# Weight halves kept in memory by block 0 and loaded by the seven later blocks

## The chip, the cores and the metric

One core of a Trainium2 chip runs the kernel. Its engines are TensorE (PE), VectorE (DVE), ScalarE (ACT), GpSimd (POOL) and SyncE (SP), which here only issues DMAs. The metric is device time in microseconds of one execution. Before the change it is 2832.45 us, the median of 3 runs (2832.03 to 2832.45).

## The reference

A layer of a streaming encoder over 4096 frames of 1024 features. All projections are in float32.

```python
mod = c_act @ ada_w[l] + ada_b[l]
shift, scale, gate = jnp.split(mod, 3, axis=-1)
h = rms_norm(x, norm_w[l]) * (1.0 + scale[:, None]) + shift[:, None]
p = h @ w_in[l]
gq, gk, gv, gz, glr, hq, hf, hi, hz, mg = jnp.split(p, IN_SPLITS, axis=-1)
# two chunked linear recurrences (64 frames a chunk) give o_g and o_h
g_a, g_b = jnp.split(jax.nn.sigmoid(mg + merge_b[l]), 2, axis=-1)
m = g_a * (o_g @ w_up_gla[l]) + g_b * (o_h @ w_up_hgrn[l])
x = x + gate[:, None] * (m @ w_out[l])
return rms_norm(x, final_norm_w)
```

`w_in` is 1024 by 5136, the two up projections are 512 by 1024 and `w_out` is 1024 by 1024. The weights are the same for every frame.

## The kernel before

The frames are cut into 8 blocks of 512. Each block walks through the same 66 slots. A slot is one piece of weights of 128 x 1024 (0.524 MB; slots 4 and 5 have 1088 columns) and the matmuls that use it: 24 of 512 columns in most slots, 48 of 272 columns in slots 4 and 5, and 12 in each of the 14 output slots 52 to 65 (`OUT0` is 52). Slots 0 to 27 are projections for the recurrences, 28 to 51 are merge gates (`MG_SLOT`) with the up projections among them (`UP_SLOT`). Smaller "hosted" matmuls for the recurrences stand between slots, mostly in slots 6 to 30.

For precision every weight w is split into two halves of the reduced type fp32r: `w_hi` is w rounded, and `w_lo` is w - `w_hi`. Activations are split in the same way, and each product is three matmuls, hi x hi, hi x lo and lo x hi (`PASSES`).

The weights pass through two sets of buffers. SyncE loads slot s into one of `RAW` = 4 buffers `w_raw` (`load_w`, L322 to L325). ScalarE copies it to `w_hi` (`split_hi`, L574), VectorE subtracts to `w_lo` (`split_lo`, L819), and TensorE reads both. The halves lie in a ring of `RING` = 3. ScalarE and VectorE therefore split slot s+3 at their own step s, just after TensorE has finished slot s (`slot_done`), and SyncE, which waits for `w_split` alone, runs some three slots ahead of TensorE and issues the raw load of slot s+4 once slot s is split. The other loads and stores of SyncE stand in the same program at fixed slots: x for the next block (`load_x`, `load_pair`), x for the residual (`xy`) and the stores of the result (`store_out`, L377).

The order of the work is written out by hand. Every engine has one in-order program, and they meet at semaphores. In ScalarE's step of a slot the copy of slot s+3 comes before most of the rest: activations, copies out of PSUM, and the small DMAs of `a_rows`, on which TensorE waits.

In block 0 GpSimd does one thing more (`out_pieces`, L473). It loads 8 pieces of `w_out`, multiplies them by the gate, forms their sums for a Strassen-like product, and stores 14 pieces to the scratch tensor `pieces` (L486). ScalarE waits for `pieces_out` in slot 21 of block 0 before it writes `o_tm`, which shares the memory of `w_b`; SyncE waits for it before the first load of a piece.

Of the kernel before, what the change touches and what calls it, by code (L numbers as in the profile page):

```python
# [14 lines left out]
P = 128  # L15
# [11 lines left out]
RAW, RING = 4, 3  # L27
SLOT_W = 4 * GW
# [13 lines left out]
OUT0 = _s  # L42
# [32 lines left out]
RAW_AT = [s % RAW if s < 20 else (s - 20) % 3 if s < 26 else (s - 26) % RAW for s in range(SLOTS)]  # L75
RAW_NTH = [RAW_AT[:s].count(RAW_AT[s]) for s in range(SLOTS)]
RAW_NEXT = [next(n for n in range(s + 1, 2 * SLOTS) if RAW_AT[n % SLOTS] == RAW_AT[s]) for s in range(SLOTS)]

# [4 lines left out]
def slot_width(s):  # L83
    return SLOT_W if GK0 <= s < I0 else 1024
# [13 lines left out]
def build(nc, x, xt, mod_in, cols, rows, w_stream, ada, out):  # L98
    fp32, f32r = mybir.dt.float32, mybir.dt.float32r
    ALU, ACT, AX = mybir.AluOpType, mybir.ActivationFunctionType, mybir.AxisListType  # L100
    NB = x.shape[0] // T

    ctx = ExitStack()
    with ctx:
# [126 lines left out]
        raw_in = [signal(f"raw_in{r}", RAW_AT.count(r) * 16) for r in range(RAW)]  # L231
        pieces = nc.dram_tensor("pieces", [PIECES, P, 1024], fp32, kind="Internal").ap()
        w_hi_done = signal("w_hi_done", SLOTS)
        w_split = signal("w_split", SLOTS)
# [86 lines left out]
        def _(sp):  # L321
            def load_w(s):  # L322
                r = RAW_AT[s]
                src = pieces[s - OUT0, :, :] if s >= OUT0 else w_stream[s, :, 0:slot_width(s)]
                sp.dma_start(w_raw[:, r, 0:slot_width(s)], src).then_inc(raw_in[r].sem, 16)  # L325
# [53 lines left out]
            def body(b, last, first=False):  # L379
                for s in range(SLOTS):  # L380
# [12 lines left out]
                    if s == 43 and not last:  # L393
# [3 lines left out]
                    if s in (50, 51) and not last:  # L397
                        sp.wait_ge(x_sq.sem, x_sq.at(b + 1, s - 47))
                        load_pair(b + 1, s - 50)
# [12 lines left out]
                    if s == 3 and not first:  # L412
                        store_out(b, -NT)
# [144 lines left out]
        def _(act):  # L558
# [10 lines left out]
            def split_hi(b, s):  # L569

                r = RAW_AT[s]
                act.wait_ge(raw_in[r].sem, raw_in[r].at(b, (RAW_NTH[s] + 1) * 16))
                n = slot_width(s)
                AF(w_hi[:, s % RING, 0:n], w_raw[:, r, 0:n], ACT.Copy).then_inc(w_hi_done.sem, 1)  # L574
# [70 lines left out]
            def body(b, last):  # L645
                link_at[0], link_at[1] = b, 0
                for s in range(SLOTS):
# [42 lines left out]
                    if not (last and s + RING >= SLOTS):  # L690
                        split_hi(b if s + RING < SLOTS else b + 1, (s + RING) % SLOTS)
# [113 lines left out]
        def _(dve):  # L805
# [10 lines left out]
            def split_lo(b, s):  # L816
                dve.wait_ge(w_hi_done.sem, w_hi_done.at(b, s + 1))
                n = slot_width(s)
                V.tensor_tensor(w_lo[:, s % RING, 0:n], w_raw[:, RAW_AT[s], 0:n],  # L819
                                w_hi[:, s % RING, 0:n].bitcast(fp32), ALU.subtract).then_inc(w_split.sem, 1)  # L820
# [138 lines left out]
            def body(b, last, first=False):  # L959
                link_at[0], link_at[1] = b, 0  # L960
                for s in range(SLOTS):
# [29 lines left out]
                    if not (last and s + RING >= SLOTS):  # L991
                        split_lo(b if s + RING < SLOTS else b + 1, (s + RING) % SLOTS)
# [167 lines left out]
        def _(pe):  # L1160
# [73 lines left out]
            def slot(b, s):  # L1234
# [4 lines left out]
                pe.wait_ge(w_split.sem, w_split.at(b, s + 1))  # L1239
# [263 lines left out]
```

## Time and profile before

| what | value |
|---|---|
| median of the runs | 2832.45 us |
| profiled execution, device time | 2831.51 us |
| its span | 2829.8 us |
| TensorE busy | 2795.2 us, 99% |
| TensorE weight load busy | 2294.9 us, 81% |
| VectorE busy | 1657.9 us, 59% |
| ScalarE busy | 1354.1 us, 48% |
| GpSimd busy | 301.5 us, 11% |
| DMA moved | 372.62 MB, mean 132 GB/s |
| HBM read, written | 345.99 MB, 24.12 MB |

The span is the time from the first to the last recorded instruction; the device time is a little longer. Busy is the time in which an engine had an instruction under way. TensorE's is the sum of overlapping matmuls, merged, so 99% says that a matmul was nearly always under way and not that each ran at full speed. The start of one matmul to the start of the next is its spacing. In the rows "w_hi" and "w_lo" stand for all buffers of the ring. In the rows that give a stretch, times are from the start of the span, and block 0 runs from 41 to 393 us.

### The profile page before, as it was taken

Reading aid. Unit: us, or ns where it says so; the run is one execution under the profiler, and the core shown is the slowest. Engines: PE = TensorE matmul, PEld = TensorE weight load, DVE = VectorE, ACT = ScalarE, POOL = GpSimd, SP = SyncE. Lnnn points to the kernel's source line nnn. Section 1 sums busy time; section 2 is a strip of 40 time slices with the busy share of each in tenths; the row PEclk is TensorE's granted clock in tenths of the full one; section 3 lists DMA queues with packets and bytes.
Section 4 is the critical chain, followed back from the end, with each engine's and each line's share of the span. In section 5 each row is a group of like instructions: output and inputs, shape, how many; then the busy total and the mean of one; then the engine's idle time right before and its main releaser. Section 6 shows DMA issues by size and latency. Waiting matters only on the chain.

```text
span 2829.8 us, 35553 instructions
## 1 busy us (share of the span) xinstructions
PE 2795.2 (99%) x14328; PEld 2294.9 (81%) x14328; DVE 1657.9 (59%) x2122; ACT 1354.1 (48%) x1763; POOL 301.5 (11%) x415
## 2 busy tenths in 40 slices
PE   6999999999999999999999999999999999999998
PEld 4878888788887888888888888888888888888886
DVE  7865475644756456564565636646376463755636
ACT  4643357434573345633456434564345643465333
POOL 1531100101001010010100110001100011000101
PEclk9999999999999999999999999999999999999999
DMA  8533363233622345323442235422354223632234
GB/s 338 203 132 102 121 224 96 76 104 128 219 87 83 105 154 190 96 75 122 166 167 91 75 127 177 152 92 73 127 187 145 89 74 127 206 123 88 82 97 149
DMA packets 100627, 372.62 MB, mean 132 GB/s; under 512 B 11440, under 2 KB 11696, under 8 KB 98928
## 3 DMA queue, kind: packets, MB, share of 16 engines
q1 hardware_dynamic: 97040, 358.62, 38.2%
q0 software_dynamic: 3168, 11.54, 1.1%
q8 instruction: 114, 1.87, 0.3%
q14 instruction: 49, 0.40, 0.0%
q10 hardware_dynamic: 256, 0.20, 0.0%
HBM read 345.99 MB, written 24.12 MB: 131 GB/s over the span
## 4 chain that ended last, share of the span: by engine, by line
PE 97%; DVE 2%; DMA 1%; SPq 0%; ACT 0%; POOL 0%; issue 0%; POOLq 0%; ACTq 0%; DVEq 0%
PE F L1230 33%; PE A L1219 32%; PE A L1281 12%; PE A L1303 9%; PE F L1219 3%; PE F L1303 2%; PE R L1333 1%; PE F L1360 1%; PE A L1375 1%; DMA ada_w<-in_ada 1%; PE F L1354 1%; PE R L1326 1%; DVE h_tmp L826 0%; DVE gates L983 0%; PE R L1168 0%; PE R L1360 0%
## 5 line engine op out<-in xcount | busy, mean ns | idle before, releaser
L819 DVE TENSOR_TENSOR w_lo<-w_raw,w_hi 128x1024 fp32r<-128x1024 f32 x528 | 661.2, 1253 | 895.9 <-ACT w_hi L574 894.7
L574 ACT ACTIVATE w_hi<-w_raw 128x1024 fp32r<-128x1024 f32 x528 | 557.2, 1057 | 660.6 <-PE A L1219 343.1
L1230 PE MATMUL F<-h_hi,w_hi 128*128 128x512 f32 x1408 | 553.8, 393 | 0.0
L1230 PE MATMUL F<-h_lo,w_hi 128*128 128x512 f32 x1408 | 548.2, 389 | 0.0
L1230 PE MATMUL F<-h_hi,w_lo 128*128 128x512 f32 x1408 | 548.1, 389 | 0.0
L1219 PE MATMUL A<-w_hi,h_hi 128*128 128x512 f32 (+1 forms) x1408 | 532.6, 378 | 0.0
L1219 PE MATMUL A<-w_lo,h_hi 128*128 128x512 f32 (+1 forms) x1408 | 523.0, 371 | 0.0
L1219 PE MATMUL A<-w_hi,h_lo 128*128 128x512 f32 (+1 forms) x1408 | 522.8, 371 | 0.0
L1230 PEld LDWEIGHTS F<-h_hi,w_hi 128*128 128x128 f32 x1408 | 264.3, 188 | 56.2 <-issue 1.7
L1219 PEld LDWEIGHTS A<-w_hi,h_hi 128*128 128x128 f32 x1408 | 264.4, 188 | 55.6 <-issue 8.7
L1230 PEld LDWEIGHTS F<-h_lo,w_hi 128*128 128x128 f32 x1408 | 264.4, 188 | 55.4 <-issue 1.7
L1230 PEld LDWEIGHTS F<-h_hi,w_lo 128*128 128x128 f32 x1408 | 264.3, 188 | 55.3
L1219 PEld LDWEIGHTS A<-w_hi,h_lo 128*128 128x128 f32 x1408 | 264.3, 188 | 46.6
L1219 PEld LDWEIGHTS A<-w_lo,h_hi 128*128 128x128 f32 x1408 | 264.7, 188 | 42.7 <-issue 0.2
L688 ACT ACTIVATE gates<-F,col 128x512 f32<-128x512 f32 x128 | 88.0, 688 | 439.2 <-PE F L1230 439.2
L1281 PE MATMUL A<-o_hi,w_hi 128*128 128x512 f32 x512 | 199.2, 389 | 0.0
L1281 PE MATMUL A<-o_lo,w_hi 128*128 128x512 f32 x512 | 199.2, 389 | 0.0
L1281 PE MATMUL A<-o_hi,w_lo 128*128 128x512 f32 x512 | 199.2, 389 | 0.0
L983 DVE TENSOR_TENSOR gates<-gates,A 128x512 f32<-128x512 f32 x128 | 82.2, 684 | 133.6 <-PE A L1281 133.6
L457 POOL TENSOR_TENSOR rstd<-ssq,eps_t 128x4 f32<-128x4 f32 x64 | 33.9, 530 | 1156.8 <-DVE ssq L1110 1156.8
L1281 PEld LDWEIGHTS A<-o_lo,w_hi 128*128 128x128 f32 x512 | 96.1, 188 | 20.0
L1281 PEld LDWEIGHTS A<-o_hi,w_hi 128*128 128x128 f32 x512 | 96.1, 188 | 20.0
(214 smaller groups left out, 3501.4 us busy)
## 6 DMA issues: line engine op xcount, KB each, us to landing
w_raw<-in_w_stream SPq DMA_DIRECT2D x400, 512.0 KB, 3.5
w_raw<-pieces SPq DMA_DIRECT2D x112, 512.0 KB, 4.0
xy<-in_x SPq DMA_DIRECT2D x32, 512.0 KB, 6.2
result<-xy SPq DMA_DIRECT2D x32, 512.0 KB, 2.7
xf<-in_xt SPq DMA_DIRECT2D x30, 512.0 KB, 5.1
xn<-in_x SPq DMA_DIRECT2D x28, 512.0 KB, 4.5
ada_w<-in_ada SPq DMA_DIRECT2D x12, 1024.0 KB, 17.5
w_raw<-in_w_stream SPq DMA_DIRECT2D x16, 544.0 KB, 5.1
```

What stands on the lines that cost most here:

```text
L457: nc.gpsimd.tensor_tensor(dst, src, eps_t[:, 0:k], ALU.add).then_inc(pool_pow, 1)
L574: AF(w_hi[:, s % RING, 0:n], w_raw[:, r, 0:n], ACT.Copy).then_inc(w_hi_done.sem, 1)
L688: AF(gates[:, j % 2, g, :], F[g][:, :], ACT.Sigmoid, bias=merge_b[:, g * KT + FEAT[j]:g * KT + FEAT[j] + 1]).then_inc(mg_used.sem, 1)
L819: V.tensor_tensor(w_lo[:, s % RING, 0:n], w_raw[:, RAW_AT[s], 0:n], w_hi[:, s % RING, 0:n].bitcast(fp32), ALU.subtract).then_inc(w_split.s ...
L983: ins = V.tensor_tensor(gates[:, j % 2, g, :], gates[:, j % 2, g, :], A[2 * (j % 2) + g][:, :], ALU.mult)
L1219: last = mm(banks[t][:, 0:width], src[ia][:, k, t * P:(t + 1) * P], w_[iw][:, s % RING, kk * width:(kk + 1) * width], start=(k == 0 and n ...
L1230: last = mm(dst[:, :], w_[iw][:, s % RING, k * P:(k + 1) * P], h_[ia][:, k, :], start=(k == 0 and n == 0), stop=(k == KT - 1 and n == 2))
L1281: last = mm(A[2 * (j % 2) + g][:, :], w_[iw][:, s % RING, kk * P:(kk + 1) * P], o_[ia][:, kk, :], start=(k == 0 and n == 0), stop=(k == HE ...
L1303: last = mm(OUT_BANK[pair_][tt][:, :], src[ia][:, 2 * (2 * q + kk) + f, at:at + P], w_[iw][:, s % RING, kk * 512:(kk + 1) * 512], start=(f ...
L1326: last = mm(R[c][r * CHUNK:(r + 1) * CHUNK, g * P:(g + 1) * P], gk[fr, t, h * CHUNK:(h + 1) * CHUNK], v_g[fr, t, h * P:(h + 1) * P], start ...
L1333: last = mm(R[c][:, g * P:(g + 1) * P], kdec_h[fr, t, g * P:(g + 1) * P], v_h[fr, t, g * P:(g + 1) * P], start=True, stop=True)
L1354: last = mm(F[r][c * CHUNK:(c + 1) * CHUNK, g * P:(g + 1) * P], q_g[dk, g, t * P + c * CHUNK:t * P + (c + 1) * CHUNK], S_g[dk, c, g, :], s ...
```

## The change

After block 0 the halves of slots 3 to 51 (`KEPT`, 49 slots) are not computed any more. In block 0 SyncE stores both halves of each such slot to a scratch tensor `halves`, behind its split (`keep_halves`), and ScalarE writes slot s+3 into the ring only when slot s has been stored (`halves_kept`). In blocks 1 to 7 SyncE loads both halves straight into the ring (`load_halves`) once TensorE has finished slot s of the ring place, and TensorE waits for `halves_in` in place of `w_split`. ScalarE and VectorE skip these splits. Slots 0 to 2 and 52 to 65 are split in every block as before, and the raw buffers go round over these uses alone (`USES`). As SyncE now waits for `slot_done` in the later blocks, its loads of x stand three slots earlier in its program there (`early`), and the stores of the result follow slot 2 in place of slot 3.

```diff
+BLOCKS = 8
+KEPT = range(RING, OUT0)
+def from_raw(b, s):
+    return b == 0 or s not in KEPT
+USES = [(b, s) for b in range(BLOCKS) for s in range(SLOTS) if from_raw(b, s)]
+USE = {v: u for u, v in enumerate(USES)}
...
+            def keep_halves(s):
+                n = slot_width(s)
+                for i, part in ((0, w_hi), (1, w_lo)):
+                    sp.dma_start(halves[s - RING, i, :, 0:n],
+                                 part[:, s % RING, 0:n].bitcast(fp32)).then_inc(halves_kept[s % RING], 16)
+            def load_halves(s):
+                n = slot_width(s)
+                for i, part in ((0, w_hi), (1, w_lo)):
+                    sp.dma_start(part[:, s % RING, 0:n].bitcast(fp32),
+                                 halves[s - RING, i, :, 0:n]).then_inc(halves_in[s % RING], 16)
...
-                    if not (last and RAW_NEXT[s] >= SLOTS):
-                        sp.wait_ge(w_split.sem, w_split.at(b, s + 1))
-                        if RAW_NEXT[s] == OUT0:
-                            sp.wait_ge(pieces_out, PIECES * 16)
-                        load_w(RAW_NEXT[s] % SLOTS)
-                    if s in (37, 38) and not last:
-                        load_x(b + 1, s - 37)
+                    if from_raw(b, s):
+                        u = USE[b, s]
+                        sp.wait_ge(w_split, u + 1)
+                        if first and s in KEPT:
+                            keep_halves(s)
+                        if u + RAW < len(USES):
+                            if USES[u + RAW] == (0, OUT0):
+                                sp.wait_ge(pieces_out, PIECES * 16)
+                            load_w(u + RAW)
+                    if not first and s + RING in KEPT:
+                        if (b, s) == (1, 0):
+                            for r in range(RING):
+                                sp.wait_ge(halves_kept[r], 32 * len([n for n in KEPT if n % RING == r]))
+                        sp.wait_ge(slot_done.sem, slot_done.at(b, s + 1))
+                        load_halves(s + RING)
+                    early = 0 if first else 3
+                    if s + early in (37, 38) and not last:
+                        load_x(b + 1, s + early - 37)
...
-                    if s == 3 and not first:
+                    if s == 2 and not first:
                         store_out(b, -NT)
...
             def split_hi(b, s):
+                u = USE[b, s]
+                r = u % RAW
+                act.wait_ge(raw_in[r], 16 * (u // RAW + 1))
+                if b == 0 and s - RING in KEPT:
+                    act.wait_ge(halves_kept[s % RING], 32 * (s // RING - 1))
...
-                pe.wait_ge(w_split.sem, w_split.at(b, s + 1))
+                if from_raw(b, s):
+                    pe.wait_ge(w_split, USE[b, s] + 1)
+                else:
+                    pe.wait_ge(halves_in[s % RING], 32 * (kept_nth(b, s) + 1))
```

The first place is SyncE's queue at the start of block 0, before:

```order
L342 DMA ada_w_89<-in_ada 128x2048 [waits modT,ada_pe]
L342 DMA ada_w_89<-in_ada 128x2048
L325 DMA w_raw<-in_w_stream 128x1088 [waits w_split] x2
L325 DMA w_raw<-in_w_stream 128x1024 [waits w_split] x36
L328 DMA xn<-in_x 128x1024
```

and the same place now, where a row `halves<-w_hi` or `halves<-w_lo` is a store:

```order
L373 DMA ada_w_89<-in_ada 128x2048 [waits modT,ada_pe]
L373 DMA ada_w_89<-in_ada 128x2048
L342 DMA w_raw<-in_w_stream 128x1088 [waits w_split] x2
L342 DMA w_raw<-in_w_stream 128x1024 [waits w_split]
L348 DMA halves<-w_hi 128x1024 [waits w_split]
L348 DMA halves<-w_lo 128x1024
L342 DMA w_raw<-in_w_stream 128x1024
L348 DMA halves<-w_hi 128x1088 [waits w_split]
L348 DMA halves<-w_lo 128x1088
L342 DMA w_raw<-in_w_stream 128x1024
```

Ahead of each raw load of slot s+4 stand two stores of slot s, from slot 3 on.

The second place is SyncE's queue from the last output slots of block 0 into block 1, up to the stores of the result (`xy_94`, `xy_95` are the tiles of the finished block), before:

```order
L325 DMA w_raw<-pieces 128x1024 [waits w_split] x5
L325 DMA w_raw<-in_w_stream 128x1024 [waits w_split] x4
L335 DMA xf<-in_xt 128x1024 [waits h_split]
L325 DMA w_raw<-in_w_stream 128x1088 [waits w_split] x2
L325 DMA w_raw<-in_w_stream 128x1024 [waits w_split] x2
L377 DMA result<-xy_94 128x1024 [waits y_ready] x2
L377 DMA result<-xy_95 128x1024 [waits y_ready] x2
```

and now, from slot 0 of block 1 to its slot 3:

```order
L342 DMA w_raw<-pieces 128x1024 [waits w_split]
L355 DMA w_hi<-halves 128x1024 [waits halves_kept2,slot_done,halves_kept1,halves_kept0]
L355 DMA w_lo<-halves 128x1024
L342 DMA w_raw<-pieces 128x1024 [waits w_split]
L355 DMA w_hi<-halves 128x1088 [waits slot_done]
L355 DMA w_lo<-halves 128x1088
L342 DMA w_raw<-pieces 128x1024 [waits w_split]
L355 DMA w_hi<-halves 128x1088 [waits slot_done]
L355 DMA w_lo<-halves 128x1088
L408 DMA result<-xy_94 128x1024 [waits y_ready] x2
L408 DMA result<-xy_95 128x1024 [waits y_ready] x2
L355 DMA w_hi<-halves 128x1024 [waits slot_done]
```

The loads wait for `slot_done` where they waited for `w_split`. At slots 0, 1 and 2 a raw load of an output piece goes ahead of each pair. The stores of the result come after the pair that waits for slot 2, and the next pair comes behind them.

The third place is ScalarE in block 0, slots 17 to 21, up to the first copy into `o_tm`, before:

```order
L683 ACTIVATE gates<-F 128x512 [waits hq_used,slot_done]
L574 ACTIVATE w_hi<-w_raw 128x1024 [waits raw_in1]
L683 ACTIVATE gates<-F 128x512 [waits hq_used,slot_done]
L574 ACTIVATE w_hi<-w_raw 128x1024 [waits raw_in2]
L574 ACTIVATE w_hi<-w_raw 128x1024 [waits raw_in0,slot_done]
L574 ACTIVATE w_hi<-w_raw 128x1024 [waits raw_in1,slot_done]
L765 ACTIVATE o_tm<-F 128x2x128 [waits o_done,pieces_out,out_stored]
L765 ACTIVATE o_tm<-F 128x2x128
```

and now:

```order
L728 ACTIVATE gates<-F 128x512 [waits hq_used,slot_done]
L619 ACTIVATE w_hi<-w_raw 128x1024 [waits halves_kept0,raw_in1]
L728 ACTIVATE gates<-F 128x512 [waits hq_used,slot_done]
L619 ACTIVATE w_hi<-w_raw 128x1024 [waits halves_kept1,raw_in2]
L619 ACTIVATE w_hi<-w_raw 128x1024 [waits halves_kept2,raw_in3,slot_done]
L619 ACTIVATE w_hi<-w_raw 128x1024 [waits halves_kept0,raw_in0,slot_done]
L811 ACTIVATE o_tm<-F 128x2x128 [waits o_done,pieces_out,out_stored]
L811 ACTIVATE o_tm<-F 128x2x128
```

The instructions are the same, and each copy to `w_hi` waits for the store of the halves that lay in its ring place too. In blocks 1 to 7 these copies are gone.

## Rows read from the trace of the kernel before

**Rows 1.** the page, busy time, and the clock in 40 slices
```profile
PE 2795.2 (99%) x14328; PEld 2294.9 (81%) x14328; DVE 1657.9 (59%) x2122; ACT 1354.1 (48%) x1763; POOL 301.5 (11%) x415
PEclk9999999999999999999999999999999999999999
```

**Rows 2.** who TensorE waited for, whole run: us in total, times, longest
```profile
PE A L1176 <- DMA ada_w<-in_ada: 16.4, 3, 8.9
PE F L1219 <- DVE h_lo L849: 4.5, 1, 4.5
```

**Rows 3.** who TensorE waited for, from 44 us to the end
```profile
PE R L1168 <- DVE h_tmp L826: 1.2, 7, 0.2
```

**Rows 4.** windows: stretch, length, busy time of each engine, clock, DMA share, GB/s
```profile
240.00:280.00 40.00, 40.00 (x178) 33.14 (x177) 15.84 (x18) 12.70 (x16) 2.95 (x4) 1.00 0.36 119
600.00:640.00 40.00, 40.00 (x178) 33.14 (x177) 14.05 (x16) 11.58 (x14) 2.94 (x4) 1.00 0.38 125
720.00:760.00 40.00, 40.00 (x178) 33.14 (x177) 33.96 (x42) 21.58 (x31) 2.97 (x8) 1.00 0.58 188
```

**Rows 5.** the chain that ended last, in order of time: start, length, what
```profile
41.07 5.46 PE F L1219 x12
49.33 2.72 PE F L1219 x12
```

**Rows 6.** groups by line and shape, the two splits: busy, mean ns, idle before
```profile
L819 DVE TENSOR_TENSOR w_lo<-w_raw,w_hi 128x1024 fp32r<-128x1024 f32 x512 | 641.2, 1252 | 884.5 <-ACT w_hi L574 883.3
L574 ACT ACTIVATE w_hi<-w_raw 128x1024 fp32r<-128x1024 f32 x512 | 540.1, 1055 | 627.3 <-PE A L1219 311.6 <-PE A L1281 180.3 <-PE A L1303 87.1
```

**Rows 7.** DMA issues: KB each, median us to landing; w_raw's range after 400
```profile
w_raw<-in_w_stream SPq DMA_DIRECT2D x400, 512.0 KB, 3.5
result<-xy SPq DMA_DIRECT2D x32, 512.0 KB, 2.7
DMA to landing us min/median/max: 3.1/3.5/7.0
```

**Rows 8.** windows in block 0: full DMA engines, the hard stretch, its fullest part
```profile
50.00:55.00 5.00, 5.00 (x24) 4.14 (x23) 3.59 (x6) 2.15 (x3) 0.00 (x0) 1.00 1.01 411
115.00:165.00 50.00, 49.98 (x225) 40.38 (x224) 40.95 (x24) 34.23 (x40) 36.41 (x27) 1.00 0.72 258
135.00:140.00 5.00, 5.00 (x22) 3.75 (x21) 3.12 (x3) 3.25 (x6) 4.68 (x3) 1.00 1.00 371
```

**Rows 9.** SyncE's queue in time, block 1: start, length, the result's stores
```profile
407.86 6.71 SPq L377 DMA_DIRECT2D result<-xy  x4
```

**Rows 10.** VectorE in time, subtracts of slots 12, 15 and 19
```profile
109.44 3.31 DVE L819 TENSOR_TENSOR w_lo<-w_raw,w_hi 128x1024 fp32r<-128x1024 f32 x1
123.77 3.43 DVE L819 TENSOR_TENSOR w_lo<-w_raw,w_hi 128x1024 fp32r<-128x1024 f32 x1
144.34 3.60 DVE L819 TENSOR_TENSOR w_lo<-w_raw,w_hi 128x1024 fp32r<-128x1024 f32 x1 [0.18 <-ACT w_hi L574]
```

**Rows 11.** ScalarE in time, the copies of slots 15, 18, 22 and 24
```profile
121.84 1.04 ACT L574 ACTIVATE w_hi<-w_raw 128x1024 fp32r<-128x1024 f32 x1
137.14 1.05 ACT L574 ACTIVATE w_hi<-w_raw 128x1024 fp32r<-128x1024 f32 x1
160.77 1.06 ACT L574 ACTIVATE w_hi<-w_raw 128x1024 fp32r<-128x1024 f32 x1
172.66 1.06 ACT L574 ACTIVATE w_hi<-w_raw 128x1024 fp32r<-128x1024 f32 x1 [5.20 <-PE A L1219]
```

**Rows 12.** TensorE in time, the first matmul of slot 12
```profile
112.95 0.39 PE L1219 MATMUL A<-w_hi,h_hi 128*128 128x512 f32 x1
```

**Rows 13.** GpSimd's queue in time, the last of 14 pieces stored
```profile
160.73 0.58 POOL L486 DMA_DIRECT2D pieces<-w_b  x1 [0.30 <-POOL w_b L514]
```

**Rows 14.** the first slot: TensorE's start, and a window with its clock
```profile
41.07 0.76 PE L1219 MATMUL F<-w_hi,h_hi 128*128 128x512 f32 x1 [4.49 <-DVE h_lo L849]
42.00:44.00 2.00, 2.00 (x6) 1.55 (x5) 0.60 (x2) 1.68 (x3) 0.00 (x0) 0.50 0.98 410
```

More of the change, by code:

```diff
@@ L72, with kept_nth @@
 assert SLOTS == 66 and SLOTS % RING == 0
-RAW_AT = [s % RAW if s < 20 else (s - 20) % 3 if s < 26 else (s - 26) % RAW for s in range(SLOTS)]
-RAW_NTH = [RAW_AT[:s].count(RAW_AT[s]) for s in range(SLOTS)]
-RAW_NEXT = [next(n for n in range(s + 1, 2 * SLOTS) if RAW_AT[n % SLOTS] == RAW_AT[s]) for s in range(SLOTS)]
+BLOCKS = 8
[4 more added lines that the diff above has]
+USE = {v: u for u, v in enumerate(USES)}
+def kept_nth(b, s):
+    per = len([n for n in KEPT if n % RING == s % RING])
+    return (b - 1) * per + (s - RING) // RING
 ADA_DVE = [5, 5, 6, 6, 8, 8]
@@ L101, in build @@
     NB = x.shape[0] // T
+    assert NB == BLOCKS
     ctx = ExitStack()
@@ L228, in build @@
         OT_BANK = A + R + A[0:2]
-        raw_in = [signal(f"raw_in{r}", RAW_AT.count(r) * 16) for r in range(RAW)]
+        raw_in = [sem(f"raw_in{r}") for r in range(RAW)]
+        halves_in = [sem(f"halves_in{r}") for r in range(RING)]
+        halves_kept = [sem(f"halves_kept{r}") for r in range(RING)]
+        halves = nc.dram_tensor("halves", [len(KEPT), 2, P, SLOT_W], fp32, kind="Internal").ap()
         pieces = nc.dram_tensor("pieces", [PIECES, P, 1024], fp32, kind="Internal").ap()
-        w_hi_done = signal("w_hi_done", SLOTS)
-        w_split = signal("w_split", SLOTS)
+        w_hi_done, w_split = sem("w_hi_done"), sem("w_split")
         slot_done = signal("slot_done", SLOTS)
@@ L396, in body @@
                             load_x(b + 1, t)
-                    if s in (50, 51) and not last:
-                        sp.wait_ge(x_sq.sem, x_sq.at(b + 1, s - 47))
-                        load_pair(b + 1, s - 50)
+                    if s + early in (50, 51) and not last:
+                        sp.wait_ge(x_sq.sem, x_sq.at(b + 1, s + early - 47))
+                        load_pair(b + 1, s + early - 50)
                     if s in (54, 65) and not last:
@@ L689, in body @@
                            bias=merge_b[:, g * KT + FEAT[j]:g * KT + FEAT[j] + 1]).then_inc(mg_used.sem, 1)
-                    if not (last and s + RING >= SLOTS):
-                        split_hi(b if s + RING < SLOTS else b + 1, (s + RING) % SLOTS)
+                    to = (b, s + RING) if s + RING < SLOTS else (b + 1, s + RING - SLOTS)
+                    if to in USE:
+                        split_hi(*to)
                     if s in UP_SLOT:
@@ L990, in body @@
                         bank_adds(b, s - OUT0)
-                    if not (last and s + RING >= SLOTS):
-                        split_lo(b if s + RING < SLOTS else b + 1, (s + RING) % SLOTS)
+                    to = (b, s + RING) if s + RING < SLOTS else (b + 1, s + RING - SLOTS)
+                    if to in USE:
+                        split_lo(*to)
                     if first and s in (1, 3):
```

19 lines of the change are left out of this document (9 added, 10 removed).

## The prediction

> **What bounds the kernel now.** I read the page's engine table and clock line first [rows 1]. TensorE is busy in 2795.2 of 2829.8 us, at a granted clock of nine tenths or more in each of the 40 slices. Busy matmuls can hide gaps, so the waits of TensorE came next [rows 2]. The reader is to see how short that list is. The large entries are 16.4 us for the adaLN weights and 4.5 us for h_lo, each before the first slot. From 44 us on, TensorE waited 1.2 us in all [rows 3]. So the 528 slots follow each other without a hole, and the time is the number of matmuls times their spacing.
>
> Is that spacing a property of TensorE, or does other traffic stretch it? Three 40 us stretches answer [rows 4]. Each holds 178 matmuls, with VectorE busy 15.84, 14.05 and 33.96 us and with 119, 125 and 188 GB/s of DMA. Twice the VectorE work and half as much DMA again changed nothing. Twelve matmuls take 2.72 us [rows 5], so one takes 0.227 us and a slot of 24 takes 5.44 us. At 50 to 55 us the DMA engines were full at 411 GB/s, and TensorE still kept its spacing [rows 8].
>
> **What is removed.** 49 slots in 7 blocks are 343 splits. Each had one ScalarE copy of 1.055 us and one VectorE subtract of 1.25 us [rows 6], so 362 us leave ScalarE and 429 us leave VectorE. Neither ends a wait of TensorE after 44 us [rows 3]. They lie wholly beside the matmuls, so their removal is worth 0 us. Next on the path is what is there already, TensorE's own spacing.
>
> **What is added in blocks 1 to 7.** A 0.524 MB raw load becomes two loads. Its buffer pair is free only when slot s is done, while the raw load could run four slots ahead. A load now stands where the 2.3 us split stood. It is due when slot s+3 starts, two slots or 10.9 us later. One such load landed after 3.5 us in the median and, from 400 us on, 7.0 us at worst [rows 7]. Two need another 0.33 us issue and 1.3 us of transfer (0.524 MB at 411 GB/s), so 5 us in the ordinary case, and from the rows I bound it by 3.5 and 8.6 us (7.0 + 0.33 + 1.3). Both ends are under 10.9. I take 5 us, nearest to the row of the same kind of load, with 6 us to spare. Cost: 0.
>
> SyncE now goes in step with TensorE, since it waits for each slot. Behind each waiting load stand the loads of x, the stores of the result and the next halves. The tightest place is after the stores of the result. In before, SyncE was held there for 6.7 us [rows 9]; now it reaches them only after slot 2, when VectorE scales the last two tiles and does nothing else, so it is through before slot 3 is done. From the end of slot 2, two halves, one raw load, four stores and the next two halves make 9 x 0.524 = 4.7 MB, or 11.5 us at 411 GB/s, plus about 2 us of landing: 13.5 us. The last two are due 16.3 us after that same moment, so 2.8 us remain. This is the least cover I find in these blocks. Were it gone, the price would be its shortfall seven times. All loads of x keep their place in time: they are issued three slots earlier in the program because SyncE no longer runs three slots ahead.
>
> **What is added in block 0.** Each of 49 slots stores 1.05 MB, behind its split, in the queue that also carries the raw loads. An ordinary slot then moves 1.57 MB in 5.44 us, 289 GB/s, under every full-load rate of the trace. The hard stretch is 115 to 165 us, where GpSimd rewrites the output weights. Before moved 258 GB/s there [rows 8]. Its slots take about 5.9 us, so the stores add 178 and the demand is 436 GB/s. Full engines gave 411 GB/s for plain loads and 371 in the mix of GpSimd's and SyncE's transfers. The excess is 25 to 65 GB/s over 50 us, 1.25 to 3.3 MB, so the queue is late by 3.0 to 8.8 us at the end of the stretch.
>
> What waits for it is ScalarE, which may write slot s+3 into the ring only when slot s is stored. Queued behind it stand its PSUM copies, activations and small DMAs, for which TensorE waits. A pair of stores needs 2.6 us of transfer and some 1.4 us more (the result's stores land in 2.7 us, 1.3 of it transfer [rows 7]), so 4 us. The room is what lies between the end of a VectorE subtract and ScalarE's copy three slots on: slot 12 ends at 112.75 and the copy starts at 121.84, 9.1 us; slot 15 gives 127.20 to 137.14, 9.9 us; slot 19 gives 147.94 to 160.77, 12.8 us [rows 10, 11]. Less 4 us this leaves 5.1, 5.9 and 8.8 us. The backlog there is at most about 0, 2.1 and 5.7 us (65 GB/s over 33 us is 2.1 MB), growing with the stretch. ScalarE then does not wait, or hardly. A second cover lies behind it: TensorE takes a slot later than its split ends. That one is thin at slot 12, whose split ends at 112.75 with its first matmul at 112.95 [rows 10, 12]; but ScalarE's copy for it needs only the store of slot 9, which is issued some four slots earlier, ahead of the hard stretch.
>
> The same backlog touches GpSimd, whose last piece is issued at 160.73 [rows 13]; ScalarE needs it landed near 173.6, just behind its copy of 172.66 [rows 11]. GpSimd waits about four times for its own transfers, so 1 to 3 us each make it 4 to 12 us later, against some 10 us of room, with a slot of TensorE behind it. I put 0 to 2 us on the path for all of block 0, lower end 0, upper end 8.8 us if none of the covers held. I take 0.5.
>
> The Trainium skill speaks against this change: "DMA: Bandwidth & Descriptors", in its anatomy of one DMA, says that a transfer's fixed time is mostly the receipt of its last write, heaviest where HBM is written. Here the rows have the stores landing in 2.7 us against 3.5 us for loads [rows 7], the other way round. By the page the room at slot 12 would shrink by perhaps the 2 us it gives for the whole fixed part, an estimate, and still be positive.
>
> **Sum.** Span 2829.8 + 0 - 0 + 0.5 = 2830.3 us. The profiled execution took 2831.51, 1.7 more than its span, and the median of the runs is 0.9 above it, so 2832.9: I say 2833.
>
> **Rivals.** A, slower: the DMA queue paces block 0. Stores mixed with loads may move less than either alone, which no long stretch of before shows. At 300 GB/s the stretch from 115 us overflows by 136 x 50 = 6.8 MB, 23 us late; about 13 us of it is covered (8.8 for ScalarE, some 4 to 5 behind it), so 10 us remain. At 270 GB/s every stored slot takes 5.83 us: 49 x 0.39 = 19 us. It decides below about 340 GB/s. TensorE would then show holes, and in the prelude a hole of 4.49 us was followed by 12 matmuls at the clock of 0.50 that took 5.46 us instead of 2.72 [rows 5, 14], so 2.7 us more. Time: 2839 to 2853. The Trainium skill ("HBM Reference", specifications) gives about 358 GB/s of HBM per core. The stretch of 411 GB/s disagrees, as far as loads go; by 358 the excess would be 3.9 MB, an estimate of 11 us late, mostly inside the covers. Chance 0.16.
>
> B, slower: the halves come late in each later block, behind the result's stores, where I find 2.8 us of room. One or two microseconds short in seven blocks is 7 to 14 us: 2840 to 2847. Chance 0.08.
>
> C, faster: the splits' traffic did slow TensorE. 512 columns at 2.4 GHz are 0.213 us against 0.227; were the rest to go in the 343 slots, 343 x 24 x 0.0134 = 110 us would, giving 2723. Equal counts under unequal VectorE load speak against it [rows 4]. Chance 0.03.
>
> **How the numbers follow.** The forecast, no change on the path, has 0.73. This kernel's times can tell 0.2%, 5.7 us, from no change. Faster is C, 0.03. Slower is A and B less their short ends, 0.21. The rest, 0.76, is the same. Below 2831 lies only C. The upper end, 2842, takes in the 8.8 us bound and the milder half of A and B.
>
> **What would show it.** Right: TensorE's waits after 44 us still near 1 us; VectorE near 1229 us busy and ScalarE near 992; HBM written near 76 MB (24 and 98 stores of 0.524) and read near 526 (346 and 343 loads of 0.524); more than 200 GB/s mean. Holes of TensorE before 200 us released by w_lo or by ScalarE, with ScalarE waiting for a DMA of halves, are A. Matmuls of slots 3 to 8 waiting for a halves load in each later block are B. More than 178 matmuls in 600 to 640 us is C. The forecast is wrong if TensorE's waits from 44 us on sum to over 6 us, or its spacing moves.

## The result and the profile after

The changed kernel took 2838.43 us (median of 14 runs, 2837.8 to 2840.63); the kernel before took 2832.39 us beside it (14 runs, 2831.29 to 2834.03). The ratio is 1.0022, interval 1.0014 to 1.0030: slower by some 6 us. The prediction said 2833 and "the same". The time is inside its range, 2831 to 2842. The change of 6.0 us is just past the 5.7 us that the prediction said can be told from none, so its likeliest case, no change on the path, did not come.

The page of the kernel after, span, busy time and memory traffic, answers to [rows 1]:

```profile
span 2836.6 us, 35194 instructions
...
PE 2797.2 (99%) x14328; PEld 2296.2 (81%) x14328; DVE 1258.9 (44%) x1779; ACT 1023.2 (36%) x1420; POOL 297.1 (10%) x415
...
HBM read 526.28 MB, written 75.63 MB: 212 GB/s over the span
```

VectorE lost 399 us of busy time and ScalarE 331, and the span grew by 6.8 us. Next, what TensorE waited for from 44 us to the end, and the place in time (start, length, what; idle before it in brackets):

```profile
PE F L1405 <- issue: 6.0, 1, 6.0
PE R L1216 <- DVE h_tmp L873: 0.2, 1, 0.2
```

```profile
178.82 0.39 PE L1267 MATMUL A<-w_hi,h_lo 128*128 128x512 f32 x1
185.25 1.13 PE L1405 MATMUL F<-S_g,q_g 64*64 64x128 f32 x16 [6.04 <-issue]
...
187.16 0.79 PE L1267 MATMUL A<-w_hi,h_hi 128*128 128x512 f32 x1
...
188.59 0.39 PE L1267 MATMUL A<-w_hi,h_hi 128*128 128x512 f32 x1
```

The reader is to see that the whole loss is one place. In [rows 3] the list held 1.2 us. Now it holds one hole of 6.04 us, from 179.21 to 185.25, at the end of slot 22 of block 0. Comparing the start of each slot's first matmul in the two traces gives the rest of the account: slot 22 is 6.99 us longer (the hole, and some 0.9 us of slower matmuls behind it), slot 23 is 0.61 longer, the other slots of block 0 do not differ, and each later block is 0.1 us shorter, because the small waits of [rows 3] are down to 0.2 us once. 6.99 + 0.61 - 7 x 0.1 = 6.9, against 6.8 in the span. About 6.1 of the 7.6 us in slots 22 and 23 are the hole; the other 1.5 are matmuls at a lower clock, which the windows below show.

What TensorE waited for is put down to "issue", so its own record does not say. ScalarE's and GpSimd's do. ScalarE in time, the copy of slot 24 and the output piece's first use; then GpSimd in time:

```profile
172.51 1.06 ACT L619 ACTIVATE w_hi<-w_raw 128x1024 fp32r<-128x1024 f32 x1 [5.20 <-PE A L1267]
184.49 0.66 ACT L811 ACTIVATE o_tm<-F 128x256 f32<-128x256 f32 x2 [10.92 <-DMA pieces<-w_b]
```

```profile
134.85 2.14 POOL L542 DMA_DIRECT2D w_b<-in_w_stream  x4 [7.84 <-DMA pieces<-w_b]
143.84 2.40 POOL L534 TENSOR_TENSOR w_b<-w_b,gate_bc 128x1024 f32<-128x1024 f32 x1 [6.84 <-DMA w_b<-in_w_stream]
...
161.72 2.95 POOL L550 TENSOR_TENSOR w_b<-w_b 128x1024 f32<-128x1024 f32 x1 [5.48 <-DMA pieces<-w_b]
...
174.95 0.58 POOL L528 DMA_DIRECT2D pieces<-w_b  x1 [0.30 <-POOL w_b L556]
```

ScalarE stood 10.92 us in front of its copy of `F` to `o_tm`, for the last of the 14 pieces that GpSimd stores. That piece was issued at 174.95, in [rows 13] at 160.73: 14.2 us later. It then took until about 184.4 to land, 9.5 us, where in the kernel before it took 3.2 us, to 163.9. GpSimd's own waits for its transfers, 7.84, 6.84 and 5.48 us, stand in the kernel before as:

```profile
129.92 2.14 POOL L500 DMA_DIRECT2D w_b<-in_w_stream  x4 [2.92 <-DMA pieces<-w_b]
134.46 2.39 POOL L492 TENSOR_TENSOR w_b<-w_b,gate_bc 128x1024 f32<-128x1024 f32 x1 [2.40 <-DMA w_b<-in_w_stream]
...
147.96 2.41 POOL L508 TENSOR_TENSOR w_b<-w_b 128x1024 f32<-128x1024 f32 x1 [1.12 <-DMA pieces<-w_b]
```

That is 13.7 us more in three waits, which is nearly all of the 14.2.

Windows of the kernel after (stretch, length, busy time of PE, PEld, DVE, ACT and POOL, clock, DMA share, GB/s):

```profile
100.00:115.00 15.00, 15.00 (x67) 12.35 (x66) 14.97 (x9) 11.40 (x10) 14.26 (x7) 1.00 0.68 249
115.00:165.00 50.00, 49.97 (x226) 40.58 (x225) 38.51 (x24) 34.45 (x40) 27.34 (x21) 1.00 1.02 396
175.00:180.00 5.00, 4.21 (x19) 3.14 (x17) 1.86 (x5) 0.00 (x0) 0.53 (x1) 1.00 1.02 406
182.00:183.00 1.00, 0.00 (x0) 0.00 (x0) 0.00 (x0) 0.00 (x0) 0.00 (x0) 0.50 1.07 438
187.00:188.00 1.00, 1.00 (x9) 0.74 (x3) 1.00 (x2) 0.93 (x3) 1.00 (x1) 0.50 0.06 25
189.00:190.00 1.00, 1.00 (x6) 0.78 (x6) 0.97 (x3) 0.46 (x1) 0.00 (x0) 1.00 1.01 406
600.00:640.00 40.00, 40.00 (x178) 33.14 (x177) 7.53 (x12) 4.65 (x7) 2.96 (x4) 1.00 0.64 225
```

These answer to [rows 4, 8]. At 60 to 80 us the DMA engines are full (364 GB/s); at 100 to 115 they have room again, a share of 0.68. In the hard stretch they are full and move 396 GB/s instead of 258; at 175 to 180, when the last piece stands in the queue, they are still full at 406. The granted clock was 1.00 ahead of the hole. It is at 0.50 (1.2 of 2.4 GHz) from 182 us on, inside the hole, and still when TensorE starts again; by 189 it is back at 1.00. The three matmuls from 187.16 to 188.59 take 1.43 us, and the same three took 0.82 in the kernel before. With the small matmuls ahead of them this makes the 1.5 us. At 600 us the 178 matmuls stand as before, with VectorE 7.53 us busy instead of 14.05 and 225 GB/s instead of 125.

The transfers of the later blocks answer to [rows 7]:

```profile
w_hi<-halves SPq DMA_DIRECT2D x329, 512.0 KB, 3.6
w_lo<-halves SPq DMA_DIRECT2D x329, 512.0 KB, 4.5
...
result<-xy SPq DMA_DIRECT2D x32, 512.0 KB, 7.9
```

The halves land in the median in about the time of the raw loads (3.5) or 1 us more. The result's stores now have the next halves around them and land in 7.9 us instead of 2.7. TensorE waited for none of it.

How near it came can be read behind the stores of each later block. The nearest is block 5: SyncE in time from the end of slot 2, and the landing of the pair of slot 6, the one behind the stores:

```profile
1802.99 0.32 SPq L355 DMA_DIRECT2D w_hi<-halves  x1
1803.83 4.78 SPq L408 DMA_DIRECT2D result<-xy  x4
...
1809.70 1.00 SPq L355 DMA_DIRECT2D w_lo<-halves  x1
...
1820.54 0.32 SPq L355 DMA_DIRECT2D w_hi<-halves  x1
```

```profile
DMA to landing us min/median/max: 7.3/8.7/10.1
```

The `w_lo` issued at 1809.70 landed 10.1 us later, at 1819.8, and slot 6 starts when slot 5 is done, at 1820.54: 0.7 us of room. In the seven later blocks this room was 0.7 to 3.3 us.

### The profile page after: what moved, and what is told of

Its sections match the earlier page's. It is cut to its first block, busy times and chain, and to the rows that moved or that the text cites. A ratio compares the mean times of both kernels' runs of the same rounds, so it can differ in the third digit from the quotient of the medians.

```text
span 2836.6 us, 35194 instructions
## 1 busy us (share of the span) xinstructions
PE 2797.2 (99%) x14328; PEld 2296.2 (81%) x14328; DVE 1258.9 (44%) x1779; ACT 1023.2 (36%) x1420; POOL 297.1 (10%) x415
## 3 DMA queue, kind: packets, MB, share of 16 engines
HBM read 526.28 MB, written 75.63 MB: 212 GB/s over the span
## 4 chain that ended last, share of the span: by engine, by line
PE 97%; DVE 1%; DMA 1%; issue 0%; ACT 0%; SPq 0%; POOL 0%; POOLq 0%; DVEq 0%; ACTq 0%
PE F L1278 33%; PE A L1267 32%; PE A L1332 12%; PE A L1354 9%; PE F L1267 3%; PE F L1354 2%; PE R L1384 1%; PE F L1411 1%; PE A L1426 1%; PE F L1405 1%; DMA ada_w<-in_ada 1%; PE R L1377 1%; DVE h_tmp L873 0%; DVE gates L1030 0%; PE R L1216 0%
## 5 line engine op out<-in xcount | busy, mean ns | idle before, releaser
L866 DVE TENSOR_TENSOR w_lo<-w_raw,w_hi 128x1024 fp32r<-128x1024 f32 x185 | 242.4, 1311 | 160.8 <-ACT w_hi L619 160.3
L619 ACT ACTIVATE w_hi<-w_raw 128x1024 fp32r<-128x1024 f32 x185 | 195.6, 1057 | 203.9 <-PE A L1354 84.9
L741 ACT ACTIVATE m_hi<-m_raw 128x512 fp32r<-128x512 f32 x64 | 40.5, 633 | 290.9 <-DVE m_raw L1034 290.9
```

Of the source, the lines that this page charges most:

```text
L741: AF(m_hi[:, j, :], m_raw[:, j, :], ACT.Copy).then_inc(m_hi_done.sem, 1)
L866: V.tensor_tensor(w_lo[:, s % RING, 0:n], w_raw[:, u % RAW, 0:n], w_hi[:, s % RING, 0:n].bitcast(fp32), ALU.subtract).then_inc(w_split, 1)
```

## Experiments

Ten kernels ran, each beside the kernel before on the same chip. Theory T1, formed from the trace above: block 0's stores fill the DMA queue, GpSimd's chain of dependent transfers comes late through it, and TensorE pays for the part beyond its cover. Rival R1: the loads of halves in the later blocks cost the time. Rival R2: ScalarE's wait for the halves' stores costs it. In the kernel after that wait is short:

```profile
ACT w_hi L619 <- DMA halves<-w_lo: 1.4, 2, 1.0
```

Five of the kernels need a table of the block in which a slot's halves are stored. It is this edit, and each names its table:

```diff
+STORED_IN = {...}
+LOADS = True
 def from_raw(b, s):
-    return b == 0 or s not in KEPT
+    return s not in STORED_IN or b <= STORED_IN[s] or not LOADS
...
-                        if first and s in KEPT:
+                        if STORED_IN.get(s) == b:
                             keep_halves(s)
```

### Stores alone, and the stretch's stores moved (e1, e2)

```diff
+STORED_IN = {s: 0 for s in KEPT}
+LOADS = False
```

> Block 0 stores the halves as in the changed kernel, but the later blocks never load them: they split all 66 slots as the kernel before does. Theory 1 (the lost time is one hole of about 6 us in slot 22 of block 0, where ScalarE waits for GpSimd's last piece of the output weights, which the stores delay): the hole stays, 6 to 7 us, and the time is 2838.4 to 2839.3 us, a ratio of 1.0021 to 1.0025. Theory 2 (the DMA queue paces block 0 as a whole): the same total, but spread over many slots. Theory 3 (the loads of the later blocks carry part of the cost): less than 2836 us.

Measured: 2840.09 us, ratio 1.0028 (1.0016 to 1.0039), 0.8 us above what T1 gave. Waits of TensorE from 44 us on:

```profile
PE F L1414 <- issue: 5.6, 1, 5.6
```

The loss is all there with no load of halves in the kernel, and blocks 1 to 7 took the time they took before. R1 falls. The converse is to move the stores of slots 10 to 21 out of the hard stretch into block 1:

```diff
+STORED_IN = {s: 1 if 10 <= s <= 21 else 0 for s in KEPT}
```

> Slots 10 to 21 store their halves in block 1 in place of block 0 (and are split once more there); the other 37 slots as in the changed kernel. Theory 1: GpSimd finds the DMA engines as in the kernel before, the hole goes, and the time is 2831 to 2833 us, a ratio of 0.9995 to 1.0002. Theory 2: 37 of 49 slots are still stored in block 0, so three quarters of the 6 us remain, 2837 us. Theory 3: no change from 2838.4 us.

Measured: 2831.13 us, ratio 0.9997 (0.9988 to 1.0005). No hole; the last piece was issued at 161.4 and used at 174.34. So the loss hangs on stores of those slots in block 0.

### The stores of the stretch and nothing else (e3): a miss

```diff
+STORED_IN = {s: 0 for s in KEPT if 10 <= s <= 21}
```

> Only slots 10 to 21 are stored in block 0 and loaded later; the other 37 kept slots are split in every block as before. Theory 1: these twelve slots are the ones that meet GpSimd's transfers, so most of the hole stays, 4 to 6 us, and the time is 2836 to 2838.5 us. Theory 2: a quarter of the stores costs a quarter, 2834 us. Theory 3: a quarter of the loads, 2834 us.

Measured: 2832.07 us, ratio 0.9998 (0.9989 to 1.0007). The expectation was wrong, and it is the run that taught most. Its GpSimd, its ScalarE, and its windows:

```profile
174.99 0.58 POOL L537 DMA_DIRECT2D pieces<-w_b  x1 [0.30 <-POOL w_b L565]
```

```profile
179.14 0.66 ACT L820 ACTIVATE o_tm<-F 128x256 f32<-128x256 f32 x2 [5.36 <-DMA pieces<-w_b]
```

```profile
115.00:165.00 50.00, 49.98 (x226) 40.59 (x225) 39.04 (x24) 34.55 (x40) 27.33 (x20) 1.00 1.02 396
175.00:180.00 5.00, 4.53 (x24) 3.45 (x26) 1.91 (x5) 0.83 (x3) 0.57 (x1) 1.00 0.66 226
```

The hard stretch is as full as in the kernel after (396 GB/s), and the last piece is issued at 174.99, as late as there. But at 175 to 180 the queue moves 226 GB/s and has room, so the piece lands in some 4 us rather than 9.5. ScalarE waits 5.36 us, and TensorE has a hole of 0.47 us. So T1 was too wide: GpSimd's 14 us alone are covered. The narrower theory T2: the hole needs the late chain *and* a queue that is still full when the last piece is issued, and it is the second that tips it.

### Is T2 right? Only the last stores moved, and only they kept (e9, e10)

```diff
+STORED_IN = {s: 1 if 20 <= s <= 24 else 0 for s in KEPT}
```

> As the changed kernel, but slots 20 to 24 store their halves in block 1. Slots 3 to 19 are still stored in block 0, so GpSimd's steps are as late as in the changed kernel; only the queue in which its last piece stands, issued near 175 us, is shorter. Theory 1 in its narrower form (what decides is when that last piece lands, with some 5 us of room in slot 22 before TensorE feels it): it lands after about 4 us in place of 9.4 us, ScalarE writes o_tm near 179 us, the hole is 0 to 1 us, and the time is 2831 to 2833 us. If the lateness that GpSimd has collected by 175 us decided by itself, the hole would stay near 6 us, 2838 us.

Measured: 2831.07 us, ratio 0.9997 (0.9989 to 1.0006). The last piece, its use, and the longer of TensorE's two waits from 44 us:

```profile
175.16 0.58 POOL L537 DMA_DIRECT2D pieces<-w_b  x1 [0.30 <-POOL w_b L565]
```

```profile
178.39 0.66 ACT L820 ACTIVATE o_tm<-F 128x256 f32<-128x256 f32 x2 [4.69 <-DMA pieces<-w_b]
```

```profile
PE R L1386 <- DVE a_cols L1137: 0.4, 1, 0.4
```

The chain is as late as in the kernel after, the piece lands in 3.2 us, and the hole is gone. ScalarE's waits for the halves' stores are as long as in the kernel after (1.3 us, against 1.4), and cost nothing here: R2 falls. Five slots' stores out of 49 carry the whole loss, given the others. The other way round:

```diff
+STORED_IN = {s: 0 for s in KEPT if 20 <= s <= 24}
```

> The counterpart of the run that held back slots 20 to 24: only these five are stored in block 0 (and loaded later), the other 44 are split in every block. Theory 1 says that the hole needs both GpSimd's steps to be late by 14 us and a full queue ahead of its last piece. Here its steps are on time up to about 160 us, so the last piece is issued at 161 to 163 us, lands before ScalarE comes to it at 173.6 us, there is no hole, and the time is 2831 to 2833 us. If the queue ahead of the last piece were enough by itself, the hole would be 3 us or more, 2835 us and up.

Measured: 2832.85 us, ratio 1.0002 (0.9993 to 1.0011). The last piece went out at 161.93. ScalarE's use of it:

```profile
175.03 0.64 ACT L820 ACTIVATE o_tm<-F 128x256 f32<-128x256 f32 x2
```

No wait stands in brackets. The piece had landed after 4.7 us, some 8 us before ScalarE came to it. So these stores cost nothing where the chain is not late. What e10 does not do is hold the piece back for the full 9.5 us: when it was issued the queue was only filling (a DMA share of 0.76 at 155 to 160 us). Even 9.5 us from 161.93 would end at 171.4, before ScalarE's use at 175.03; that is an estimate from the two runs, not a run. With it neither half does it alone, and T2 stands. e9 and e2 are the best of the changed versions (ratio 0.9997 each): 7 us below the kernel after, and not to be told from the kernel before.

Where the cover ends can be read across these runs: the piece was used at 178.39 with no hole there (e9), at 179.14 with a hole of 0.47 (e3), and at 184.49 with 6.04 (after). Both holes put the limit near 178.5 (179.14 - 0.47 = 178.67, 184.49 - 6.04 = 178.45).

### GpSimd's chain loosened (e5): a miss

GpSimd's work is reordered, so that each of its four buffers has a semaphore of its own and it waits for one buffer and not for all stores:

```diff
-                    pool.dma_start(pieces[piece, :, :], w_b[:, i, :]).then_inc(pieces_out, 16)
+                    pool.dma_start(pieces[piece, :, :], w_b[:, i, :]).then_inc(b_out[i], 16)
+
+                def free(i):
+                    pool.wait_ge(b_out[i], 16 * kept[i])
...
```

> The changed kernel with all its stores and loads; only GpSimd's rewriting of the output weights is reordered. Each of its four buffers has a semaphore of its own for its stores and is loaded again as soon as its own stores have landed, and the gated product of the third buffer is made later, so that fewer of its steps wait for a transfer. The values are the same. Theory 1: the second round starts 8 to 12 us earlier than in the changed kernel (143.8 us), the last piece lands before ScalarE comes to it at 173.6 us or a few microseconds later, the hole is 0 to 2 us, and the time is 2831.5 to 2834 us. Theories 2 and 3: 2838 us, nothing of the stores and loads is changed.

Measured: 2836.41 us, ratio 1.0016 (1.0007 to 1.0025). The hole at slot 22 went: the last piece was issued at 171.2 and landed at 178.5, and ScalarE, itself some 6 us later than in the kernel before, came to it at 179.6 and did not wait. Three others came. TensorE's waits from 44 us, and ScalarE's wait for a store from 150 us:

```profile
PE R L1396 <- DVE a_cols L1147: 2.1, 1, 2.1
PE F L1297 <- DVE q_h L1041: 1.9, 1, 1.9
PE R L1469 <- DVE pk L1132: 1.0, 1, 1.0
```

```profile
ACT w_hi L637 <- DMA halves<-w_lo: 5.8, 1, 5.8
```

They lie at 136.7, 156.4 and 170.1. GpSimd's tensor operations now stand beside other work of VectorE. One of VectorE's, in e5 and then in the kernel after:

```profile
128.92 3.44 DVE L1126 SCALAR_TENSOR_TENSOR y_g<-y_g,t 128x1024 f32<-128x1024 f32 x1
```

```profile
129.35 1.21 DVE L1107 SCALAR_TENSOR_TENSOR y_g<-y_g,t 128x1024 f32<-128x1024 f32 x1
```

The same instruction takes 3.44 us instead of 1.21. It starts at 128.92, and in e5 a `TENSOR_TENSOR` of GpSimd runs from 128.42 to 131.28, 2.36 us past that start; the extra time is 2.23 us. In the kernel after GpSimd ran nothing at this moment. The Trainium skill ("SBUF — State Buffer", "Who interferes with whom") says that a VectorE operation with two SBUF inputs contends with a GpSimd operation that reads SBUF, and that the port pair is an exclusive lock, the later one waiting for the whole of the other. The trace agrees with it. What e5 shows is that mending one chain moved the loss to other places; which part of the three holes is the port and which is ScalarE's 5.8 us for the store (it ended at 171.37, beside the third hole), I did not separate.

### Is the spacing TensorE's own? (e4)

This kernel leaves out the weight work of blocks 1 to 7: it stores no halves, and there neither splits nor loads slots 3 to 51, so that their matmuls run on what lies in the ring.

```diff
-                        if first and s in KEPT:
-                            keep_halves(s)
...
-                        load_halves(s + RING)
```

> Left out: block 0 stores nothing, and from block 1 on the weights of slots 3 to 51 are neither split nor loaded, so TensorE multiplies with whatever lies in the ring; all matmuls are there. It asks what the change could have given at best. If TensorE's own spacing sets the time, the removed splits are worth nothing and the time is that of the kernel before, 2831 to 2833 us, a ratio of 0.9993 to 1.0003. If the splits or the weight traffic slowed TensorE, the time falls, by up to 110 us were the spacing to go from 0.227 to 0.213 us.

Measured: 2831.69 us, ratio 0.9998 (0.9989 to 1.0007). Its window at 600:

```profile
600.00:640.00 40.00, 40.00 (x178) 33.10 (x178) 6.74 (x11) 5.34 (x8) 2.95 (x4) 1.00 0.09 27
```

178 matmuls in 40 us with 27 GB/s, as with 125 and with 225. With nearly all traffic gone nothing is gained, so rival C's gain does not exist here, and a change that only frees VectorE, ScalarE or DMA in these blocks has nothing to win.

### How much the cover in the later blocks holds (e8)

```diff
-                    if not first and s + RING in KEPT:
+                    if not first and s + RING - 1 in KEPT and s:
...
-                        load_halves(s + RING)
+                        load_halves(s + RING - 1)
```

> The changed kernel with every load of halves issued one slot later, so that it is due one slot of 5.44 us after its issue and not two slots, 10.9 us. It measures the cover in the later blocks. A pair lands 4.5 us (median) after its second issue, which comes 0.4 us behind the first, so an ordinary slot has some 0.5 us left; behind a load of x (1.3 us of transfer) it is about 0.8 us late, and behind the four stores of the result some 3 us. That is about 5 us a block, 35 us in all: 2855 to 2880 us. If the loads do not share the queue in this way, the holes are absent and the time stays 2838 us, and then the two slots of the changed kernel hold more room than they need.

Measured: 2881.56 us, ratio 1.0174 (1.0160 to 1.0188), 1.6 us above the upper end that was expected. Waits of TensorE from 44 us:

```profile
PE A L1267 <- DMA w_lo<-halves: 23.2, 16, 2.6
PE F L1405 <- issue: 5.5, 1, 5.5
```

A load one slot later makes TensorE wait in every later block. 14 of the 16 waits in the first row are at slots 4 and 5, whose pairs stand around the result's stores; the longest is 2.6 us. So a slot of cover is not spare, and the loads do share the queue with the stores. The run does not give the cover of the kernel after by subtraction (5.44 - 2.6 = 2.8): slots 4 and 5 take 6.05 us and not 5.44, and a hole at slot 4 gives slot 5's load time. The trace of the kernel after gives it directly, 0.7 to 3.3 us. The later blocks together took some 40 us more than in the kernel after, and the whole list of waits names 27 of them. Part of the rest is the clock, which is at 0.53 for 2 us after one hole of 2.4 us; the remainder I cannot place. The 5.5 us of slot 22 in block 0 are in this list too, untouched, as they must be.

### What the queue can carry (e6, e7)

The halves of slots 26 to 51 stored a second time in block 0, one of the two (e6) or both (e7). e6:

```diff
+                    if s >= 26 and i < 1:
+                        sp.dma_start(spare[s - RING, i, :, 0:n],
+                                     part[:, s % RING, 0:n].bitcast(fp32)).then_inc(spare_out[s % RING], 16)
```

> The changed kernel, with w_hi of slots 26 to 51 stored twice in block 0 (the second time to another scratch tensor), and ScalarE waits for both. An ordinary slot then moves 2.10 MB in 5.44 us, 385 GB/s, and with x some 410. If the engines give 411 GB/s in a mixture of stores and loads too, no slot after 26 is late and the time stays 2838 to 2840 us. If a mixture gives 371 GB/s or less, each slot needs 5.7 us, 0.3 x 24 = 7 us more than 5.44, some of it covered: 2840 to 2845 us, with ScalarE waiting for stores.

Measured: 2838.78 us, ratio 1.0022 (1.0012 to 1.0032), the kernel after's. Its window at 280, block 0, three stores and one load a slot:

```profile
280.00:320.00 40.00, 40.00 (x178) 33.15 (x177) 14.29 (x16) 16.09 (x23) 6.34 (x10) 1.00 1.02 409
```

The engines are full at 409 GB/s, with 178 matmuls and no hole behind slot 26. e7:

```diff
-                    if s >= 26 and i < 1:
+                    if s >= 26 and i < 2:
```

> The changed kernel, with both halves of slots 26 to 51 stored twice in block 0, and ScalarE waits for all. It asks where the queue does pace block 0. A slot now moves 2.62 MB and the run with three stores moved 409 GB/s without a hole, so a slot needs 6.4 us in place of 5.44: in slots 31 to 51 21 x 1.0 us, and the loads of x (8 x 0.524 MB) add some 10 us, 31 us in all. The covers take about 13 us of it (9 us until ScalarE waits, some 5 behind it), so some 12 to 20 us remain, in holes after slot 35, with ScalarE waiting for stores: 2850 to 2858 us. If the covers are deeper, less than 2845 us.

Measured: 2861.25 us, ratio 1.0103 (1.0089 to 1.0117), 3 us above the upper end that was expected. Its windows, TensorE's waits from 44 us, ScalarE's waits from 190, and ScalarE's copy ahead of the longest hole:

```profile
320.00:360.00 40.00, 29.36 (x113) 22.67 (x111) 12.37 (x15) 11.82 (x17) 4.78 (x11) 0.88 1.02 410
340.00:345.00 5.00, 4.31 (x10) 3.44 (x11) 1.24 (x2) 2.26 (x5) 0.74 (x2) 0.50 1.02 407
```

```profile
PE R L1223 <- DVE h_tmp L880: 7.1, 1, 7.1
```

```profile
ACT w_hi L626 <- DMA spare<-w_lo: 48.8, 12, 6.4
```

```profile
357.04 1.06 ACT L626 ACTIVATE w_hi<-w_raw 128x1024 fp32r<-128x1024 f32 x1 [5.18 <-DMA spare<-w_lo]
```

Five transfers of 0.524 MB in 5.44 us ask for 482 GB/s; 410 were served. Here rival A's mechanism is seen at work: ScalarE waited 48.8 us for stores, and block 0 took 30.3 us more than in the kernel before. The longest hole, 7.1 us, comes from the same wait. VectorE does its subtract, a small operation on `m_lo` and then `h_tmp` in order, and the subtract had waited for the copy at 357.04, which had stood 5.18 us for a store of `spare`. TensorE's waits behind slot 22 sum to 14.4 us, inside the 12 to 20 that were expected. What the expectation left out is the clock: it stood at 0.50 behind the holes of 3.3 and 7.1 us. From the clock rows this costs some 6 us more, an estimate, and together they give about 20 of the 22.8 us over the kernel after. So a mixture of stores and loads moves 409 to 410 GB/s, what plain loads moved in [rows 8]; the queue paces block 0 when more than that is asked for (e7), and not yet at 409 (e6). Rival A had put the border near 340.

## Where the prediction held and where it failed

**What held.** TensorE's spacing bounds the kernel, and the 343 splits were worth nothing: 178 matmuls at 600 us, with or without them (after, e4). The loads of halves cost nothing: e1 loses as much without them. The traffic is as counted: 526.28 MB read and 75.63 written, 212 GB/s. All loss lies in block 0. Of the busy times, VectorE came to 1258.9 and not 1229, ScalarE to 1023.2 and not 992: a split took 399/343 = 1.16 us off VectorE's busy time, not the 1.25 of its duration, and 331/343 = 0.96 off ScalarE's, not 1.055. The groups' own sums fell by 418.8 and 361.6 us, but busy time counts once what overlaps with another instruction of the engine. It costs nothing here, but a group's mean times its count overstates what an engine gets back.

**The step that failed** is the term for block 0, put at 0 to 2 us on the path and taken as 0.5, and in it the sentence on GpSimd: "GpSimd waits about four times for its own transfers, so 1 to 3 us each make it 4 to 12 us later, against some 10 us of room". The right chain was named, with the right room (some 10 us and a slot of TensorE behind it). What the runs show in its place is a landing of the last piece 20.5 us later against 14.6 us of room, which left the hole of 6.04 us, and 1.5 us of low clock behind it. Five things in the sizing were off.

- The price of a wait. 1 to 3 us each was a guess that no row carried. Three waits came 4.9, 4.4 and 4.4 us later, 13.7 together. A transfer of 0.5 MB issued by GpSimd lands in 8.4 us in the median (4.0 before).
- The last transfer was not counted. After the last piece is issued, it has to land in the same queue. That took 9.5 us against 3.2, so it landed 14.2 + 6.3 = 20.5 us later. In the kernel before it had landed at 163.9, and the cover ended near 178.5, 14.6 us behind. e3 and e9 show that the first 14.2 alone cost 0 to 0.5 us. The 6.3 are what makes the hole.
- Two numbers of the same text did not meet. The backlog had been worked out as 3.0 to 8.8 us at the end of the stretch, from an excess of 25 to 65 GB/s. The stretch then moved 396 of the 436 GB/s asked for, an excess of 40 that gives 2 MB, or 5 us: inside the range named, and the queue did have room ahead of 115 us. (This is an estimate: with GpSimd late, not all of the 436 was asked for in the stretch.) But GpSimd's transfers stand in the same queue, and were charged 1 to 3 us. Had the three waits and the last landing each been given that 5 us, the chain would have come 3 x 5 + 5 = 20 us late.
- The sum stopped at 165 us. Slots 22 to 24 go on storing behind the stretch, and so nothing empties the queue before the last piece has landed. By e3 and e9 this is the difference between 0 and 6 us.
- The clock behind a hole was priced in rival A (2.7 us) and not in the forecast's own sum. It took 1.5 us here.

The upper bound, 8.8 us "if none of the covers held", did hold the 7 us, and that kept the time inside the range. That is partly luck: the bound was the backlog of ScalarE's queue at the end of the stretch, and the time was lost in another chain, by another sum. The chance did not follow the bound: a step with 4 to 12 us against 10 has no right to 0.5 us and 0.76.

**The second cover** was there, as named, but it was less than was needed: ScalarE waited 10.92 us and TensorE stood for 6.04, so it held 4.9 us.

**Rival B's room** was put at 2.8 us, "the least cover I find in these blocks". The place was right and no block ran out, but the sum was not: behind the stores the pair landed up to 16.8 us after the end of slot 2 and not 13.5, and it was due 17.5 us after and not 16.3, since slots 4 and 5 take 6.05 us. The least room was 0.7 us. So it was a nearer thing than the prediction says that none of the seven blocks lost time.

**Rival A** came nearest in time (2839 to 2853) but not in mechanism. Its sign, ScalarE waiting for stores of halves ahead of TensorE's hole, is not what stands there. It put the loss on the rate of mixed transfers and on ScalarE's wait for stores of halves. That rate is 396 to 409 GB/s, and ScalarE's wait for those stores was 1.4 us in two pieces in the kernel after. The Trainium skill ("HBM Reference", "Specifications (TRN2)") gives about 358 GB/s as a core's share with both cores of a pair streaming, and about 425 for a core that streams alone. One core runs here, and the 409 to 411 GB/s measured are nearer the second, so the stretch of 411 does not disagree with the page, as the prediction had it; its sum by 358 used the figure of the other case. Nor does a dearer write explain the loss: a store in a queue with room (e9, the last piece) landed in 3.2 us, the same store in a full one in 9.5.

**Its own sign of failure** was given as waits over 6 us after 44 us. They sum to 6.2, at the place and by the engine it had named last.

## What to carry to other kernels

Added traffic that fills DMA engines which had room is paid for by every chain that issues a transfer and waits for it: count one queueing delay (here 4.4 to 4.9 us) for each step of the chain, and one more for the landing of its last transfer (here 6.3). Do the sum for the moment when that last transfer is issued, not for the stretch's mean, and spread a one-time cost to a place without such a chain: moving five slots' stores by one block took back all 7 us (e9). And where an engine on the path is at its own spacing, ask what work removed beside it could give before asking what it costs; here the answer was nothing (e4).

## What was not expected of the hardware

- Stores and loads mixed moved 409 GB/s over 40 us (e6) and 410 (e7), no less than plain loads. 371 GB/s in [rows 8] had suggested less.
- The wait of one engine's transfer behind another engine's traffic is large: GpSimd's transfers of 0.5 MB went from 4.0 to 8.4 us in the median and to 14.8 at most, while SyncE's own loads of halves in the later blocks had a median of 4.3 us, and 10.3 at most.
- In the hole of 6.04 us, and in those of 3.3 and 7.1 us of e7, the granted clock went to 0.50, and it was still there when TensorE started again. After holes of 2.4 and 2.6 us in e8 it was once at 0.53 and once at 1.00, and after the hole of 0.47 us (e3) at 1.00.
- VectorE's operation of 1.21 us took 3.44 us beside one of GpSimd (e5).
